# Two weight stages of a decoder trunk: w_out with its recurrent half first in three tiles, w_pg with four accumulators

## The chip, the cores and the metric

The kernel runs on one core of one Trainium2 chip. The metric is the device time of one execution in microseconds. TensorE is called PE, VectorE DVE, ScalarE ACT, GpSimd POOL and SyncE SP, as in the profile.

## The reference, cut to what matters

One layer, 264 tokens (256 of a prompt, 8 of a sample group), width 2048:

```python
c = silu(layernorm(causal_dw_conv(u)))            # channels 0 to 1023
r_out = rg_lru(lx) * gelu(l_gate)                 # channels 1024 to 2047
h = h + concatenate([c, r_out], axis=-1) @ w_out
h = h + hier_moe(rmsnorm(h, norm2_g), ...)        # 32 experts, top 2 of 8 in one of 4 groups
gate = sigmoid(rmsnorm(h, ple_norm_g) @ w_pg + b_pg)
h = h + gate * (p @ w_ple)
y = rmsnorm(h, final_g)
```

The change lies in the product with w_out and in the product with w_pg, both 2048 x 2048.

## The kernel before, in words

The stages follow each other: the input product w_in (PE tiles 0 to 31), w_out (tiles 32 to 47, `CT_OUT`), router, w_ple, 32 experts, w_pg (`CT_PG`), final norm. Every engine's program is written out by hand, in order, with semaphores between engines.

w_out and w_pg are worked alike. Output is made in 16 tiles of 128 channels. The weights of tile t (128 x 2048 floats, 1 MB) are loaded by SP into one of four slots (`lo_slot`), ACT rounds them into another of four slots (`round_weights`, L1105, counted by `w_hi_ready`), and DVE leaves the rest, weight minus rounded weight, in the first slot (`rest_weights`, L1420, counted by `w_lo_ready`). The activations are split the same way (`x_hi`, `mix_lo` for w_out; `gx_hi`, `gx_lo` for w_pg). A tile is then 48 matmuls, three for each of 16 blocks k: high x high, high x low, low x high (`split_product`, L790 to L792). Accumulators are PSUM banks n % 3. SP loads weight tile t once the product of tile t-4 is done (L473, L509).

w_out: `MIX_ORDER` takes the recurrent blocks 8 to 14, then the conformer blocks 0 to 7, then 15. For blocks 0 to 7 ACT still has to do `silu` (L1148) and then the rounding (L1160), and DVE the low part (L1458); PE waits for `mix_lo_ready` block by block in tile 0. DVE's `rest_weights(2)` stands behind all 16 low parts. After each tile DVE adds it to hT (L1479) and PE does `logits` (L811) and `turn_rows` (L637, L638).

w_pg: tile m = 0 and 1 are done in passes (all high x high, then low x high, then high x low; L762, L766, L772). ACT rounds tile 16 (m = 0), makes `gx_hi` with tile 17's rounding in between, rounds tile 18, then makes 16 squares (L1238) that POOL adds up (L553). PE sums them over the channels (L1029, `sum3_full`), from which DVE and ACT make the norm's factor `rb3`. Then, for each m, DVE has one iteration: z = accumulator x rb3 (L1703, `z3_ready`); `rest_weights(KD + m + 3)`, which waits for ACT's rounding, which stands behind ACT's sigmoid (L1252) of z; z x pleT (L1707); hT + z (L1708, `h3_ready`); `take_back(m - 3)` (L1694, L1696, `y_taken`). PE after split_product m does `turn_back(m - 3)`, the transposes (L637, L638) that take_back reads; turn_back(b) waits for h3 of b and, from b = 2 on, for `y_taken` b - 1, that is take_back(b - 2). ACT also squares the new hT (L1248), and POOL adds the squares up.

The lines of the w_pg stage on PE before are these:

```python
for m in range(2, KD):
    if m >= 3:
        pe.wait_ge(z3_ready, m - 3 + 1)
    split_product(KD + m, CT_PG + m, GATE_ORDER, None)
    if m >= 3:
        turn_back(m - 3)
```

Of the kernel before, what the change touches and what calls it, by code (L numbers as in the profile page):

```python
# [17 lines left out]
TOK = SEQ + NB  # L18
# [21 lines left out]
MIX_ORDER = list(range(TC, KD - 1)) + list(range(TC)) + [KD - 1]  # L40
# [62 lines left out]
def build(nc, a, o):  # L103
# [265 lines left out]
    w_lo_ready = sem("w_lo_ready")  # L369
    mix_hi_ready = sem("mix_hi_ready")  # L370
# [148 lines left out]
    def _(pool):  # L519
# [113 lines left out]
    def _(pe):  # L633
# [123 lines left out]

        def high_high(t, n, ks, ready):
            for i, k in enumerate(ks):
                if ready:  # L760
                    pe.wait_ge(ready, i + 1)
                pe.matmul(ps[:, n % 3, 0:TOK], ring_r[:, hi_slot(t), k, :], gate_hi(t)[:, k, :], start=(i == 0), stop=False)  # L762

        def low_high(t, n, ks):
            for k in ks:
                pe.matmul(ps[:, n % 3, 0:TOK], ring_r[:, lo_slot(t), k, :], gate_hi(t)[:, k, :], start=False, stop=False)  # L766

        def high_low(t, n, ks, ready):
# [13 lines left out]
        def split_product(t, n, ks, ready):  # L782

            out = ps[:, n % 3, 0:TOK]
            pe.wait_ge(w_lo_ready, t + 1)
            for i, k in enumerate(ks):
                if ready:
                    pe.wait_ge(ready, i + 1)
                w_hi, w_lo = ring_r[:, hi_slot(t), k, :], ring_r[:, lo_slot(t), k, :]
                pe.matmul(out, w_hi, gate_hi(t)[:, k, :], start=(i == 0), stop=False)  # L790
                pe.matmul(out, w_hi, gate_lo(t)[:, k, :], start=False, stop=False)  # L791
                mm = pe.matmul(out, w_lo, gate_hi(t)[:, k, :], start=False, stop=(i == KD - 1))  # L792
            mm.then_inc(acc_full, 1)
# [29 lines left out]

        for m in range(KD):
            n = CT_OUT + m
            if m < 3:
                pe.wait_ge(acc_free, n - 3 + 1)
            else:
                pe.wait_ge(h_added, m - 3 + 1)
            split_product(m, n, MIX_ORDER, mix_lo_ready if m == 0 else None)  # L830
            if m >= 1:
                logits(m - 1)
                turn_rows(m - 1)
            if m in (2, 4, 6):
                turn_tails(m // 2 - 1)
            if m in (8, 9):

                k = m - 8
                if k == 0:
                    pe.wait_ge(p_loaded, 32)  # L840
                    pe.wait_ge(tail_taken, 3)
                else:
                    pe.wait_ge(pT_ready, 1)
                for c in range(3):
                    r = ROWS[c]
                    last = pe.transpose(ps[:, 5, c * P:c * P + r], prow[0:r, c, k * P:(k + 1) * P], ident[0:r, 0:r])
                last.then_inc(p_turned, 1)
# [174 lines left out]
        pe.wait_ge(w_hi_ready, KD + 2)  # L1022
# [5 lines left out]
        pe.wait_ge(sq3_summed, KD)  # L1028
        pe.matmul(ps[:, 7, 0:TOK], ones[:, :], acc3[:, :], start=True, stop=True).then_inc(sum3_full, 1)  # L1029
        for m in range(2, KD):  # L1030
            if m >= 3:
                pe.wait_ge(z3_ready, m - 3 + 1)
            split_product(KD + m, CT_PG + m, GATE_ORDER, None)
            if m >= 3:
                turn_back(m - 3)
        turn_back(KD - 3)
        turn_back(KD - 2)
        turn_back(KD - 1)
# [9 lines left out]
    def _(act):  # L1048
# [178 lines left out]
        for i, k in enumerate(GATE_ORDER):  # L1227
# [22 lines left out]
        for m in range(KD):  # L1250
# [3 lines left out]
            if m + 3 < KD:  # L1254
                round_weights(KD + m + 3)
# [12 lines left out]
    def _(dve):  # L1268
# [191 lines left out]
        rest_weights(2)  # L1460
# [214 lines left out]
        rest_weights(KD)  # L1675
        for i, k in enumerate(GATE_ORDER):
# [22 lines left out]
        for m in range(KD):  # L1699
# [9 lines left out]
            if m >= 3:  # L1709
                take_back(m - 3)  # L1710
# [69 lines left out]
```

## Time and profile before

| | |
|---|---|
| median of 3 runs | 1581.22 us (1580.81 to 1581.28) |
| the profiled execution's own time | 1583.43 us |
| its span, first to last instruction | 1581.6 us |
| PE busy | 1482.3 us, 94% |
| DVE, ACT, POOL busy | 618.0, 249.5, 129.2 us |
| w_out stage, first to last tile | from 285.7 to about 412 us |
| experts | from about 432 to 1444 us |
| w_pg stage and the end | from about 1444 us |

All positions are microseconds from the span's start. A row of the timeline gives start, length, engine, line, operation, output and inputs with shapes, how often, and in brackets how long the engine sat idle before it and what ended that. A run of equal instructions is merged into one row. A row of a table of stretches gives, for each engine, busy time and number of instructions, then the granted TensorE clock as a share of full speed and what the DMA moved. Matmuls are pipelined, so that the distance between two starts tells their pace, not the length shown.

### The profile page before, as it was taken

Reading aid. Unit: us, or ns where it says so; the run is one execution under the profiler, and the core shown is the slowest. Engines: PE = TensorE matmul, PEld = TensorE weight load, DVE = VectorE, ACT = ScalarE, POOL = GpSimd, SP = SyncE. Lnnn points to the kernel's source line nnn. Section 1 sums busy time; section 2 is a strip of 40 time slices with the busy share of each in tenths; the row PEclk is TensorE's granted clock in tenths of the full one; section 3 lists DMA queues with packets and bytes.
Section 4 is the critical chain, followed back from the end, with each engine's and each line's share of the span. In section 5 each row is a group of like instructions: output and inputs, shape, how many; then the busy total and the mean of one; then the engine's idle time right before and its main releaser. Section 6 shows DMA issues by size and latency. Waiting matters only on the chain.

```text
span 1581.6 us, 18598 instructions
## 1 busy us (share of the span) xinstructions
PE 1482.3 (94%) x7733; PEld 850.6 (54%) x7733; DVE 618.0 (39%) x1230; ACT 249.5 (16%) x414; POOL 129.2 (8%) x116
## 2 busy tenths in 40 slices
PE   6999998999999999999999999999999999998996
PEld 4888887788763333333433433333343333335885
DVE  4698743644552222222222222222222222226665
ACT  3100155633300000000000000000000000004432
POOL 2000000233000000000000000000000000002332
PEclk9999999999999999999999999999999999998998
DMA  9845340345469999999999999999999999991551
GB/s 288 261 147 199 106 107 1 87 134 154 182 260 422 421 421 421 418 411 409 413 405 414 413 403 414 413 409 407 413 413 403 412 415 409 408 372 46 160 160 56
DMA packets 149855, 482.70 MB, mean 305 GB/s; under 512 B 8313, under 2 KB 90785, under 8 KB 99682
## 3 DMA queue, kind: packets, MB, share of 16 engines
q1 hardware_dynamic: 148426, 475.46, 77.6%
q0 software_dynamic: 912, 2.89, 0.6%
q10 hardware_dynamic: 432, 3.15, 0.5%
q8 instruction: 62, 1.02, 0.3%
q14 instruction: 23, 0.19, 0.0%
HBM read 479.06 MB, written 3.42 MB: 305 GB/s over the span
## 4 chain that ended last, share of the span: by engine, by line
PE 85%; DVE 7%; ACT 4%; issue 2%; POOL 1%; DMA 1%; DVEq 0%; ACTq 0%; SPq 0%; POOLq 0%
PE ps L936 29%; PE ps L962 16%; PE ps L662 15%; PE ps L916 8%; PE ps L953 3%; PE ps L943 2%; PE ps L790 2%; PE ps L792 2%; PE ps L791 2%; ACT ring_r L1105 2%; DVE ring_r L1420 2%; DVE hT L1645 1%; DVE sgl L1631 1%; POOL acc L553 1%; PE ps L638 1%
## 5 line engine op out<-in xcount | busy, mean ns | idle before, releaser
L936 PE MATMUL ps<-ring,xwin 128*64 128x512 f32 x1984 | 451.4, 597 | 0.0
L1645 DVE TENSOR_TENSOR hT<-hT,ps 128x528 f32<-128x528 f32 x256 | 168.7, 700 | 394.6 <-PE ps L916 394.6
L936 PEld LDWEIGHTS ps<-ring,xwin 128*64 128x64 f32 x1984 | 133.2, 137 | 263.2 <-issue 263.2
L962 PE MATMUL ps<-ring,hid 128*64 128x512 f32 x1024 | 259.1, 664 | 0.0
L662 PE MATMUL ps<-xT,ring 128*128 128x264 f32 x1024 | 234.7, 391 | 0.0
L662 PEld LDWEIGHTS ps<-xT,ring 128*128 128x128 f32 x1024 | 197.6, 193 | 34.7
L962 PEld LDWEIGHTS ps<-ring,hid 128*64 128x64 f32 x1024 | 78.2, 157 | 153.4 <-issue 152.7
L916 PE MATMUL ps<-sel,ysb 64*128 64x264 f32 x1024 | 149.1, 409 | 1.5 <-DVE ysb L1637 0.8
L916 PEld LDWEIGHTS ps<-sel,ysb 64*128 64x128 f32 x1024 | 87.9, 186 | 112.4 <-issue 100.6
L1637 DVE COPY ysb<-ps 128x512 f32<-128x512 f32 x32 | 22.1, 692 | 287.1 <-PE ps L962 287.1
L1200 ACT ACTIVATE sgl<-ps 64x512 f32<-64x512 f32 x32 | 18.9, 589 | 548.2 <-PE ps L936 548.2
L605 POOL COPY xwin<-xTs 128x1024 f32 x31 | 32.4, 1047 | 879.9 <-PE ps L936 857.0
L1280 DVE SCALAR_TENSOR_TENSOR mix<-U,vT,mix 128x256 f32<-128x256 f32 x240 | 95.3, 475 | 0.0
L1420 DVE TENSOR_TENSOR ring_r<-ring,ring_r 128x2048 fp32r<-128x2048 f32 x32 | 73.7, 2306 | 33.9 <-ACT ring_r L1105 33.3
L943 PE MATMUL ps<-ident,sgl 64*128 64x64 f32 x256 | 35.3, 278 | 54.0 <-DVE sgl L1631 54.0
L790 PE MATMUL ps<-x_hi,ring_r 128*128 128x264 f32 x256 | 76.0, 297 | 3.4 <-DVE mix_lo L1458 3.3
L792 PE MATMUL ps<-x_hi,ring_r 128*128 128x264 f32 x256 | 73.3, 286 | 0.0
L791 PE MATMUL ps<-mix_lo,ring_r 128*128 128x264 f32 x256 | 73.2, 286 | 0.0
L1105 ACT ACTIVATE ring_r<-ring 128x2048 fp32r<-128x2048 f32 x32 | 61.0, 1906 | 47.1 <-DMA ring<-in_w_out_dram 46.7
L790 PE MATMUL ps<-gx_hi,ring_r 128*128 128x264 f32 x224 | 66.0, 295 | 2.2 <-DVE ring_r L1420 2.2
L943 PEld LDWEIGHTS ps<-ident,sgl 64*128 64x128 f32 x256 | 30.8, 187 | 67.1 <-DVE sgl L1631 67.1
L791 PE MATMUL ps<-gx_lo,ring_r 128*128 128x264 f32 x224 | 64.2, 287 | 0.0
(318 smaller groups left out, 1271.8 us busy)
## 6 DMA issues: line engine op xcount, KB each, us to landing
ring<-in_w_gate_dram SPq DMA_DIRECT2D x128, 1024.0 KB, 10.8
ring<-in_w_up_dram SPq DMA_DIRECT2D x128, 1024.0 KB, 9.1
ring<-in_w_down_dram SPq DMA_DIRECT2D x128, 1024.0 KB, 8.1
ring<-in_w_in_dram SPq DMA_DIRECT2D x32, 512.0 KB, 8.7
ring<-in_w_in_dram SPq DMA_DIRECT2D x16, 1024.0 KB, 8.0
ring<-in_w_out_dram SPq DMA_DIRECT2D x16, 1024.0 KB, 5.9
ring<-in_w_pg_dram SPq DMA_DIRECT2D x16, 1024.0 KB, 6.0
ring<-in_w_ple_dram SPq DMA_DIRECT2D x2, 1024.0 KB, 5.8
```

What stands on the lines that cost most here:

```text
L662: mm = pe.matmul(ps[:, n % 3, 0:TOK], w, rhs[:, k, :], start=(k == 0), stop=(k == kt - 1))
L790: pe.matmul(out, w_hi, gate_hi(t)[:, k, :], start=(i == 0), stop=False)
L791: pe.matmul(out, w_hi, gate_lo(t)[:, k, :], start=False, stop=False)
L792: mm = pe.matmul(out, w_lo, gate_hi(t)[:, k, :], start=False, stop=(i == KD - 1))
L916: mm = pe.matmul(ps[:, 4 + 2 * (u % 2) + half, 0:TOK], ysb[rows, b, i * P:(i + 1) * P], sel[rows, :], start=True, stop=True)
L936: mm = pe.matmul(ps[part * WIN:(part + 1) * WIN, 0, :], window(k), weights(2 * j + part)[:, kk * F:(kk + 1) * F], start=(k == 0), stop=(k ...
L943: mm = pe.matmul(ps[:, 1, t * WIN:(t + 1) * WIN], sgl[WIN:2 * WIN, t * P:(t + 1) * P], ident[WIN:2 * WIN, WIN:2 * WIN], start=True, stop=True)
L962: mm = pe.matmul(ps[half * WIN:(half + 1) * WIN, 2 + b, :], hid[:, t, :], weights(8 + t)[:, q * 512:(q + 1) * 512], start=(t == 0), stop=( ...
L1105: act.activation(ring_r[:, hi_slot(t), :, :].rearrange("p k c -> p (k c)"), ring[:, lo_slot(t), :], ACT.Copy).then_inc(w_hi_ready, 1)
L1280: return dve.scalar_tensor_tensor(out=out, in0=in0, scalar=s, in1=in1, op0=op0, op1=op1)
L1420: dve.tensor_tensor(lo, ring[:, lo_slot(t), :], hi.bitcast(F32), ALU.subtract).then_inc(w_lo_ready, 1)
L1645: dve.tensor_tensor(pair, pair, ps[:, b:b + 2, 0:TOK], ALU.add).then_inc(sems["added"], 1)
```

## The change

In w_out, PE takes the blocks 8 to 14 (`MIX_FIRST`) of tiles 0, 1 and 2 first, in passes, in three accumulators, and then the remaining blocks (`MIX_REST`) tile by tile. DVE does rest_weights(2) after the first seven low parts. In w_pg there are four accumulators (banks 0, 1, 2, 6). POOL rounds weight tiles 17 and 18 before the squares; ACT rounds tile 19 among the squares, and tile 20 and later after the sigmoid of m = t - 20. DVE does the rests of 16 and 17 before the low parts, of 18 and 19 after them, and in iteration m of the rest ahead of tile m + 4 comes after z x pleT and hT + z. The sum over the squares stands behind product m = 3. turn_back starts behind product 4, with two behind product 5 (`BACK`).

```diff
+POOL_ROUNDS = (KD + 1, KD + 2)
+BACK = {4: (0,), 5: (1, 2), **{m: (m - 3,) for m in range(6, KD)}}
+MIX_FIRST = list(range(TC, KD - 1))
+MIX_REST = list(range(TC)) + [KD - 1]
...
@@ pool
         pool.sem_inc(extra_done, 1)
+        for i, t in enumerate(POOL_ROUNDS):
+            pool.wait_ge(*landed("tile", t))
+            pool.wait_ge(main["used"], used_chunk(NCH - 9 + t % PG_SLOTS))
+            pool.tensor_copy(ring_r[:, hi_slot(t), :, :].rearrange("p k c -> p (k c)"), ring[:, lo_slot(t), :])\
+                .then_inc(w_hi_pool, 1)
...
@@ tensor
+        def acc_bank(n):
+            return n % 3 if n < CT_PG else (0, 1, 2, 6)[(n - CT_PG) % 4]
...
+        for m in range(2):
+            pe.wait_ge(acc_free, CT_OUT + m - 3 + 1)
+            first_high(m, CT_OUT + m)
+        for m in range(2):
+            first_low(m, CT_OUT + m)
+        pe.wait_ge(acc_free, CT_OUT)
+        first_high(2, CT_OUT + 2)
+        first_low(2, CT_OUT + 2)
         for m in range(KD):
             n = CT_OUT + m
             if m < 3:
-                pe.wait_ge(acc_free, n - 3 + 1)
+                rest_product(m, n)
             else:
                 pe.wait_ge(h_added, m - 3 + 1)
-            split_product(m, n, MIX_ORDER, mix_lo_ready if m == 0 else None)
+                split_product(m, n, MIX_ORDER, None)
...
-        pe.wait_ge(sq3_summed, KD)
-        pe.matmul(ps[:, 7, 0:TOK], ones[:, :], acc3[:, :], start=True, stop=True).then_inc(sum3_full, 1)
         for m in range(2, KD):
-            if m >= 3:
-                pe.wait_ge(z3_ready, m - 3 + 1)
+            if m >= 4:
+                pe.wait_ge(z3_ready, m - 4 + 1)
             split_product(KD + m, CT_PG + m, GATE_ORDER, None)
-            if m >= 3:
-                turn_back(m - 3)
-        turn_back(KD - 3)
-        turn_back(KD - 2)
-        turn_back(KD - 1)
+            if m == 3:
+                pe.wait_ge(sq3_summed, KD)
+                pe.matmul(ps[:, 7, 0:TOK], ones[:, :], acc3[:, :], start=True, stop=True).then_inc(sum3_full, 1)
+            for b in BACK.get(m, ()):
+                turn_back(b)
+        for m in range(KD - 3, KD):
+            turn_back(m)
...
@@ scalar
-            if i == 3:
-                round_weights(KD + 1)
         act.dma_start(ring[:, FING_SLOT, :], a["final_g"].partition_broadcast(P)).then_inc(fing_loaded, 16)
-        round_weights(KD + 2)
         for i, k in enumerate(GATE_ORDER):
             if i >= 2:
                 act.wait_ge(sq3_summed, i - 1)
             act.activation(sqt[:, i % 2, :], hT[:, k, :], ACT.Square).then_inc(sq3_ready, 1)
+            if i == 3:
+                round_weights(KD + 3)
...
-            if m + 3 < KD:
-                round_weights(KD + m + 3)
+            if m + 4 < KD:
+                round_weights(KD + m + 4)
...
@@ vector
+            if i == len(MIX_FIRST) - 1:
+                rest_weights(2)
...
         rest_weights(KD)
+        rest_weights(KD + 1)
         for i, k in enumerate(GATE_ORDER):
             dve.wait_ge(gx_hi_ready, i + 1)
             stt(gx_lo[:, k, :], hT[:, k, :], vT[:, V_PN + k:V_PN + k + 1], gx_hi[:, k, :].bitcast(F32),
                 ALU.mult, ALU.subtract).then_inc(gx_lo_ready, 1)
-            if i == 3:
-                rest_weights(KD + 1)
         rest_weights(KD + 2)
+        rest_weights(KD + 3)
...
-            dve.tensor_tensor(zt[:, m % 2, :], ps[:, (CT_PG + m) % 3, 0:TOK], rb3[:, :], ALU.mult).then_inc(z3_ready, 1)
-            if m + 3 < KD:
-                rest_weights(KD + m + 3)
+            dve.tensor_tensor(zt[:, m % 2, :], ps[:, (0, 1, 2, 6)[m % 4], 0:TOK], rb3[:, :], ALU.mult).then_inc(z3_ready, 1)
             dve.wait_ge(sig_ready, m + 1)
             link(dve.tensor_tensor(zt[:, m % 2, :], zt[:, m % 2, :], pleT[:, m, :], ALU.mult))
             dve.tensor_tensor(hT[:, m, :], hT[:, m, :], zt[:, m % 2, :], ALU.add).then_inc(h3_ready, 1)
-            if m >= 3:
-                take_back(m - 3)
+            if m + 4 < KD:
+                rest_weights(KD + m + 4)
+            for b in BACK.get(m, ()):
+                take_back(b)
```

`first_high`, `first_low` and `rest_product` are the three parts of a tile's product: high x high and low x high over blocks 8 to 14; high x low over them; all three over the other blocks.

## Rows read from the trace of the kernel before

**Rows 1.** Chain that ended last, from 1436 us on, shares by line
```profile
by line: ACT ring_r L1105 20.7%; DVE ring_r L1420 20.4%; POOL acc L553 9.1%; issue 8.3%; DVE zt L1707 7.8%; ACT gx_hi L1229 4.3%; DVE zt L1703 3.6%; DVE ring L1694 3.1%; PE ps L790 1.5%; DVE ring L1696 1.4%; PE ps L792 1.3%; PE ps L791 1.3%
```

**Rows 2.** Timeline, the first three w_out tiles, ACT, DVE and PE
```profile
284.67 2.29 ACT L1160 ACTIVATE x_hi<-mix 128x264 fp32r<-128x264 f32 x7
285.16 2.49 DVE L1458 TENSOR_TENSOR mix_lo<-mix,x_hi 128x264 fp32r<-128x264 f32 x7
...
285.73 0.36 PE L790 MATMUL ps<-x_hi,ring_r 128*128 128x264 f32 x1 [1.47 <-DVE mix_lo L1458]
...
290.21 0.39 PE L790 MATMUL ps<-x_hi,ring_r 128*128 128x264 f32 x1 [1.68 <-DVE mix_lo L1458]
...
295.63 2.29 DVE L1420 TENSOR_TENSOR ring_r<-ring,ring_r 128x2048 fp32r<-128x2048 f32 x1
...
302.23 0.64 PE L811 MATMUL ps<-hT,wr 128*36 128x264 f32 x2
...
303.47 0.39 PE L790 MATMUL ps<-x_hi,ring_r 128*128 128x264 f32 x1
...
309.53 0.64 PE L811 MATMUL ps<-hT,wr 128*36 128x264 f32 x2
```

**Rows 3.** Table of stretches, the start of w_out, PE alone
```profile
285.70:290.20 4.50, 2.81 (x21) 1.00 0.23 60
...
291.10:294.40 3.30, 3.30 (x13) 0.50 0.00 0
```

**Rows 4.** Timeline, low parts and their matmuls in w_pg
```profile
1447.24 1.70 DVE L1280 SCALAR_TENSOR_TENSOR gx_lo<-hT,vT,gx_hi 128x264 fp32r<-128x264 f32 x4
...
1451.06 10.54 DVE L1280 SCALAR_TENSOR_TENSOR gx_lo<-hT,vT,gx_hi 128x264 fp32r<-128x264 f32 x12
...
1462.70 2.88 PE L772 MATMUL ps<-gx_lo,ring_r 128*128 128x264 f32 x13
```

**Rows 5.** Chain in order of time, from the sum to the rest
```profile
1466.79 0.72 PE ps L1029 x2
...
1470.30 0.44 DVE zt L1703
...
1471.29 1.81 ACT ring_r L1105
1473.12 2.29 DVE ring_r L1420
```

**Rows 6.** Timeline, PE in w_pg
```profile
1475.56 0.56 PE L790 MATMUL ps<-gx_hi,ring_r 128*128 128x264 f32 x1 [2.25 <-DVE ring_r L1420]
...
1483.01 0.38 PE L637 MATMUL ps<-ident,hT 128*128 128x128 f32 x2
...
1483.64 0.39 PE L790 MATMUL ps<-gx_hi,ring_r 128*128 128x264 f32 x1
...
1489.55 0.38 PE L637 MATMUL ps<-ident,hT 128*128 128x128 f32 x2
...
1564.47 0.38 PE L637 MATMUL ps<-ident,hT 128*128 128x128 f32 x2
```

**Rows 7.** Table of stretches, w_pg: PE, PEld, DVE, ACT, POOL, clock, DMA
```profile
1475.60:1479.00 3.40, 3.40 (x16) 3.40 (x17) 0.98 (x4) 2.40 (x3) 0.00 (x0) 0.52 0.88 250
```

**Rows 8.** The page, POOL's window copies
```profile
L605 POOL COPY xwin<-xTs 128x1024 f32 x31 | 32.4, 1047 | 879.9 <-PE ps L936 857.0
```

**Rows 9.** Timeline, POOL's additions beside DVE's work
```profile
310.60 2.42 POOL L553 TENSOR_TENSOR acc<-acc,sqh 128x264 f32<-128x264 f32 x1 [3.40 <-ACT sqh L1180]
...
312.33 0.48 DVE L1468 TENSOR_TENSOR h_lo<-ps,h_hi 128x128 fp32r<-128x128 f32 x2
...
1533.20 2.55 POOL L553 TENSOR_TENSOR acc<-acc,sqt 128x264 f32<-128x264 f32 x1 [4.36 <-ACT sqt L1248]
...
1535.05 0.98 DVE L1707 TENSOR_TENSOR zt<-zt,pleT 128x264 f32<-128x264 f32 x1
```

**Rows 10.** The page, DMA issues of w_pg, median us to landing
```profile
ring<-in_w_pg_dram SPq DMA_DIRECT2D x16, 1024.0 KB, 6.0
```

More of the change, by code:

```diff
@@ L39 @@
 PG_SLOTS = 4
-MIX_ORDER = list(range(TC, KD - 1)) + list(range(TC)) + [KD - 1]
+POOL_ROUNDS = (KD + 1, KD + 2)
+BACK = {4: (0,), 5: (1, 2), **{m: (m - 3,) for m in range(6, KD)}}
+MIX_FIRST = list(range(TC, KD - 1))
+MIX_REST = list(range(TC)) + [KD - 1]
+MIX_ORDER = MIX_FIRST + MIX_REST
 GATE_ORDER = [k for u in range(KD // 2) for k in (u, u + KD // 2)]
@@ L369, in build @@
     w_lo_ready = sem("w_lo_ready")
+    w_hi_pool = sem("w_hi_pool")
     mix_hi_ready = sem("mix_hi_ready")
@@ L761, in high_high @@
                     pe.wait_ge(ready, i + 1)
-                pe.matmul(ps[:, n % 3, 0:TOK], ring_r[:, hi_slot(t), k, :], gate_hi(t)[:, k, :], start=(i == 0), stop=False)
+                pe.matmul(ps[:, acc_bank(n), 0:TOK], ring_r[:, hi_slot(t), k, :], gate_hi(t)[:, k, :], start=(i == 0), stop=False)
         def low_high(t, n, ks):
             for k in ks:
-                pe.matmul(ps[:, n % 3, 0:TOK], ring_r[:, lo_slot(t), k, :], gate_hi(t)[:, k, :], start=False, stop=False)
+                pe.matmul(ps[:, acc_bank(n), 0:TOK], ring_r[:, lo_slot(t), k, :], gate_hi(t)[:, k, :], start=False, stop=False)
         def high_low(t, n, ks, ready):
@@ L771, in high_low @@
                     pe.wait_ge(ready, i + 1)
-                mm = pe.matmul(ps[:, n % 3, 0:TOK], ring_r[:, hi_slot(t), k, :], gate_lo(t)[:, k, :], start=False,
+                mm = pe.matmul(ps[:, acc_bank(n), 0:TOK], ring_r[:, hi_slot(t), k, :], gate_lo(t)[:, k, :], start=False,
                                stop=(i == KD - 1))
@@ L782, in split_product @@
         def split_product(t, n, ks, ready):
-            out = ps[:, n % 3, 0:TOK]
+            out = ps[:, acc_bank(n), 0:TOK]
             pe.wait_ge(w_lo_ready, t + 1)
@@ L792, in split_product, with first_high, first_low, rest_product @@
                 mm = pe.matmul(out, w_lo, gate_hi(t)[:, k, :], start=False, stop=(i == KD - 1))
+            mm.then_inc(acc_full, 1)
+        def first_high(t, n):
+            pe.wait_ge(w_hi_ready, t + 1)
+            for i, k in enumerate(MIX_FIRST):
+                if t == 0:
+                    pe.wait_ge(mix_hi_ready, i + 1)
+                pe.matmul(ps[:, acc_bank(n), 0:TOK], ring_r[:, hi_slot(t), k, :], x_hi[:, k, :], start=(i == 0), stop=False)
+            pe.wait_ge(w_lo_ready, t + 1)
+            for k in MIX_FIRST:
+                pe.matmul(ps[:, acc_bank(n), 0:TOK], ring_r[:, lo_slot(t), k, :], x_hi[:, k, :], start=False, stop=False)
+        def first_low(t, n):
+            for i, k in enumerate(MIX_FIRST):
+                if t == 0:
+                    pe.wait_ge(mix_lo_ready, i + 1)
+                pe.matmul(ps[:, acc_bank(n), 0:TOK], ring_r[:, hi_slot(t), k, :], mix_lo[:, k, :], start=False, stop=False)
+        def rest_product(t, n):
+            out = ps[:, acc_bank(n), 0:TOK]
+            for i, k in enumerate(MIX_REST):
+                if t == 0:
+                    pe.wait_ge(mix_lo_ready, len(MIX_FIRST) + i + 1)
+                w_hi, w_lo = ring_r[:, hi_slot(t), k, :], ring_r[:, lo_slot(t), k, :]
+                pe.matmul(out, w_hi, x_hi[:, k, :], start=False, stop=False)
+                pe.matmul(out, w_hi, mix_lo[:, k, :], start=False, stop=False)
+                mm = pe.matmul(out, w_lo, x_hi[:, k, :], start=False, stop=(i == len(MIX_REST) - 1))
             mm.then_inc(acc_full, 1)
@@ L1021, in _ @@
         low_high(KD, CT_PG, GATE_ORDER)
-        pe.wait_ge(w_hi_ready, KD + 2)
+        pe.wait_ge(w_hi_pool, 1)
         high_high(KD + 1, CT_PG + 1, GATE_ORDER, None)
@@ L1415, in rest_weights @@
         def rest_weights(t):
-            dve.wait_ge(w_hi_ready, t + 1)
+            if t in POOL_ROUNDS:
+                dve.wait_ge(w_hi_pool, POOL_ROUNDS.index(t) + 1)
+            else:
+                dve.wait_ge(w_hi_ready, t + 1 if t <= KD else t + 1 - len(POOL_ROUNDS))
             lo = ring_r[:, lo_slot(t), :, :].rearrange("p k c -> p (k c)")
@@ L1459, in _ @@
                 .then_inc(mix_lo_ready, 1)
-        rest_weights(2)
+            if i == len(MIX_FIRST) - 1:
+                rest_weights(2)
         def rows_low(m):
```

## The prediction

> **What bounds the kernel now.** I read the page first: PE is busy for 94% of the span, so time is won or lost where PE waits, or where it runs at the lower clock. Then I read the two stages that the change touches, first by the chain of work that ended last, then by the timeline of each engine, then by a table of stretches for the granted clock.
>
> At the start of w_out PE does 21 matmuls of blocks 8 to 14 and then idles, because ACT's silu and rounding and DVE's low part give one conformer block after another [rows 2]. After that hole the granted clock is 0.50, the 1.2 GHz level, from 291.1 to 294.4 us; before it, it was 1.00 [rows 3]. The first three products run from 285.73 to 309.5 us.
>
> In w_pg the chain is not PE's: ACT's rounding and DVE's rest of the weights hold 41% of it, POOL's additions 9% [rows 1]. PE could do a tile in 6.54 us (1483.01 to 1489.55, 48 matmuls and one turn_back) [rows 6], but from 1489.55 to 1564.47 it did 11 tiles in 74.9 us, 6.81 each: DVE's iteration (z, wait for sigmoid and rounding, rest, three additions, take_back) is longer than PE's. Before that PE stood 2.25 us in front of product m = 3, because rest_weights(19) came only behind z(0) [rows 5, 6].
>
> **The terms.** A product of 48 matmuls at the high clock takes 5.91 us (1483.64 to 1489.55), a turn_back 0.63, together 6.54 [rows 6]. A product after a stall takes 1483.01 - 1475.56 = 7.45 us; its extra 1.5 us is the 3.4 us at granted clock 0.52 [rows 6, 7]. From the start of the sum's matmul to z(0) it is 1470.30 - 1466.79 = 3.5 us, and from z(0) to the end of the rest that follows it 1475.41 - 1470.30 = 5.1 us [rows 5]. This last term is the core of a DVE iteration in both kernels: z, ACT's sigmoid, ACT's rounding, DVE's rest.
>
> **w_out.** PE no longer waits for low parts at its start, but for x_hi, whose first comes about 0.4 us after 284.67, so PE begins near 285.2. Its first seven matmuls are paced by ACT, 2.29 / 7 = 0.33 each against 0.12, which costs 1.3 us [rows 2]. Then 56 matmuls of the first blocks are there without a wait (DVE's seven low parts end at 287.65, its rest of tile 2 now at about 289.9 instead of 297.8), which lasts to about 294. DVE had the low parts of the other nine blocks done by 295.63, when its rest of tile 2 began; PE asks for the last of them 8 x 0.37 us after 294, at 297, so they come in time [rows 2]. The sum: 285.2 + 1.3 + 3 x 5.91 + 1.24 (logits and turn_rows after tile 1, 302.23 to 303.47) = 305.4 us for the end of product 2, against 309.5 [rows 2]. The gain is 4.1 us. What is late next: tile 0 ends 1 us later, so the load of weight tile 4 is issued at about 297.7; with 6.0 us of landing [rows 10], 1.8 of rounding and 2.3 of rest [rows 5] it stands near 308, while PE needs it only after product 3, near 314.5. Queued behind that rest on DVE is hT + product 2, done near 308.8, before PE's turn_rows(2) asks for it. If ACT's slow first seven matmuls let the clock fall, 1.5 us of it goes; the gain cannot be above 4.9 us, the whole excess of 23.8 us over 3 x 5.91 + 1.24. Bounds 2.4 to 4.5, I take 4.1. Its cover is in PE's own queue, so it is passed on whole: what follows (router chain, expert loads gated by these tiles) starts from PE.
>
> **POOL's two roundings** are 128 x 2048; the nearest row is a copy of 128 x 1024 in 1.05 us [rows 8], so about 2.1 us each, doubled if they are blocked. They wait for their loads and for slots that expert 31 has used, so they run during expert 31, and PE asks for the first only at its third pass, after 1448. Behind them on POOL stand only the squares. What they can cost is DVE's gate of expert 31: 0 to 1 us, I take 0.
>
> **w_pg up to product 3.** ACT is rid of two roundings of 1.8 us [rows 5], so gx_hi is complete 1.8 us earlier and the squares begin 3.6 us earlier, with tile 19's rounding put between. DVE now does both rests, the first until 1447.2 as before, the second until 1449.5, and then 16 low parts. Four of them without POOL beside them took 1.70 us, 12 with it 10.54, 0.88 each [rows 4]. So 16 take 13 to 14 us and end at about 1463.3 instead of 1461.5. PE has them paced, its clock is at 0.50 again, and the last 16 matmuls take 16 x 0.22 = 3.5 us [rows 4] (2.0 at the high clock): product m = 2 begins at about 1466.8 (1465.2 at best), against 1467.15. The wait for the sum, which began at 1466.79 [rows 5], is gone from here, but the low parts take its place. Products 2 and 3 need the rests of 18 and 19, ready at 1465.6 and 1468, and run through: 1466.8 + 2 x 5.91 = 1478.6.
>
> **w_pg, product 4** (positions here leave w_out's gain aside)**.** Only now comes the sum's matmul, and z(0) is at 1478.6 + 3.5 = 1482.1, 11.8 us later than before. Product 4 waits for z3 of 0 and, worse, for the rest of tile 20. ACT rounds that tile behind the sigmoid of z(0), DVE leaves its rest behind hT + z(0). So it stands at 1482.1 + 5.1 = 1487.2, and PE has idled for 7.9 us since its sum. The fourth accumulator doesn't help: the weights are not there.
>
> **w_pg, turn_back(2).** Products 4 and 5 take 7.45 + 0.63 + 5.91 from 1487.3, to 1501.3; turn_back(1) to 1501.9. turn_back(2) then waits for take_back(0). That one stands in DVE's iteration 4, behind rest_weights(24), and DVE has been working off iterations 0 to 3 since z(0), 5.1 us each, since z(m + 1) stands behind the rest of tile m + 4. So take_back(0) ends at 1482.1 + 5 x 5.1 + 0.6 = 1508.2, and PE idles another 6.3 us. Product 6 ends at 1508.2 + 0.1 + 0.63 + 7.45 = 1516.4, again with 1.5 us of low clock. (The low clock of product 4 costs nothing: it lies inside this wait.)
>
> Does POOL lengthen these iterations? After a rest, POOL's waiting addition goes first and DVE's next operation takes 0.98 instead of 0.43, where both its inputs are in SBUF; where one is in PSUM (312.33, while POOL's addition ran from 310.60 to 313.02) it isn't lengthened [rows 9]. In the new order the operation after the rest is z or take_back, which read PSUM, so I take 0; the upper bound is 4 x 0.55 = 2.2 us. The Trainium skill, page "SBUF — State Buffer", section "Who interferes with whom", says that a DVE instruction with at most one SBUF input does not contend with GpSimd. The two rows agree; by the opposite reading the sum would be 2 us more.
>
> **w_pg, the rest.** From there PE is the slower one. DVE's iteration, 5.1 + 0.6, is shorter than PE's 6.54. A load is issued at the end of product m and lands 6.0 us later [rows 10], then rounding 1.8, rest 2.3, take_back 0.6 to 1.1: DVE's z(m + 1) runs at most 5 us behind PE, and turn_back asks for take_back(m - 5) about 2 us after it is done. Nine tiles at 6.54 to 6.6: 59.1, so the last product ends at 1575.5, against 1564.47 [rows 6]. The end behind it is the same in both kernels: turn_backs 12 to 15, last sum, last scaling. w_pg: +11.0 us. Where DVE's shorter iteration gives back: 11 x 0.27 = 3 us, already in this.
>
> **Sum.** -4.1 + 11.0 = +6.9 us. On the span of 1581.6 that is 1588.5. The profiled execution took 1583.43, the median of the three runs is 1581.22; the predicted median is 1581.2 + 6.9 = 1588.1.
>
> **Rivals.**
> B. The wait of turn_back(2) isn't there, only that of product 4 (if DVE got through its iterations much faster than 5.1 us, or PE were held elsewhere by as much). Then product 6 ends at 1501.9 + 0.63 + 5.91 = 1508.4, the last at 1567.5: +3.0 - 4.1 = -1.1, 1580.1. For it: nothing but the promise of slack; against: the order in the code, and 5.1 us from a row. 0.09.
> C. Faster: products 4 and on never wait, PE goes at its own pace from 1466.8: 14 x 5.91 + 12 x 0.63 + 0.7 = 91.0, last product at 1557.8, -6.7 - 4.1 = -10.8, 1570.4. It decides on the rest of tile 20: if it were ready before 1479. Against it: its rounding stands behind z(0) [rows 5]. Anything that makes the kernel faster by 3.2 us needs both stalls together (14.2 us, and 1.5 of clock) to be under about 6. 0.04.
> D. More than forecast: POOL does lengthen every iteration (+2.2), the clock falls in w_out (+1.5), the roundings on POOL hold expert 31's gate (+1): 1590 to 1593. 0.12.
> A. The forecast, 1585 to 1590.5: 0.75.
>
> **Range.** Low: product 2 at 1465.2 (-1.6), w_out 4.5 (-0.4), no low clock after the second stall (-1.5) give 1584.6. High: D's 1592.8. I give 1584.4 to 1592.8; B and C and ends beyond hold less than 0.2. A measurement of this kernel can tell about 0.2% (3.2 us) from no change: slower 0.87, same 0.09, faster 0.04.
>
> **What the changed profile would show.** w_out: PE with no idle over 0.5 us between 287 and 305, clock 1.00, tile 2's product ending near 305.4. Against the start of w_pg, on PE: a wait of about 8 us for DVE's rest (L1420's successor) in front of product 4; a wait of about 6 us at the transposes between products 5 and 6, released by DVE's take_back, followed by a few us at half clock; then a period of 6.5 to 6.6 us. DVE: five iterations of 5.1 us after z(0). The prediction is wrong if the second wait is missing or short, if z(0) comes before 1476 in the place where I have 1482.1 (all these positions less 4.1 us in the changed kernel, for w_out), or if periods after product 6 stay at 6.9.

## The result and the profile after

The changed kernel takes 1588.93 us, median of 5 runs (1588.44 to 1589.5), against 1581.28 (5 runs, 1580.81 to 1582.05): a ratio of 1.0047, 95% interval 1.0033 to 1.0062, or 7.65 us more. The forecast was 1588.1 us, 6.9 more. The profiled execution took 1588.82 us, with a span of 1587.1 against 1581.6.

From the page of the kernel after: the span, the busy time (us, share, instructions), and the group of the first matmul of each block k of a w_pg product (busy us, mean ns, then idle time before it and what ended it):

```profile
span 1587.1 us, 18599 instructions
PE 1480.3 (93%) x7733; PEld 849.2 (54%) x7733; DVE 614.9 (39%) x1230; ACT 246.0 (16%) x412; POOL 130.9 (8%) x118
L803 PE MATMUL ps<-gx_hi,ring_r 128*128 128x264 f32 x224 | 67.1, 300 | 8.0 <-DVE ring_r L1471 8.0
```

PE is busy for 2 us less and the span is 5.5 us longer, so PE stands idle for 7.5 us more. The waits from 1430 us on (engine and line that wait, what for, us in total, times, longest) hold two large ones on PE:

```profile
PE ps L803 <- DVE ring_r L1471: 8.0, 1, 8.0
PE ps L647 <- DVE ring L1748: 7.3, 2, 5.4
```

The first is product 4 waiting for the rest of tile 20, the second (5.4 us of it) is turn_back(2) waiting for take_back(0); the other 1.9 us is the end's, as before. The timeline of DVE after, from the low parts to take_back(0):

```profile
1440.04 4.70 DVE L1471 TENSOR_TENSOR ring_r<-ring,ring_r 128x2048 fp32r<-128x2048 f32 x2 [0.44 <-issue]
1444.66 13.46 DVE L1328 SCALAR_TENSOR_TENSOR gx_lo<-hT,vT,gx_hi 128x264 fp32r<-128x264 f32 x16
1458.05 5.03 DVE L1471 TENSOR_TENSOR ring_r<-ring,ring_r 128x2048 fp32r<-128x2048 f32 x2
1475.16 0.43 DVE L1736 TENSOR_SCALAR rbt<-ps 128x264 f32<-128x264 f32 x1 [12.08 <-PE ps L1083]
...
1477.92 0.43 DVE L1755 TENSOR_TENSOR zt<-ps,rb 128x264 f32<-128x264 f32 x1
1478.93 0.43 DVE L1757 TENSOR_TENSOR zt<-zt,pleT 128x264 f32<-128x264 f32 x1 [0.58 <-ACT zt L1300]
1479.40 0.43 DVE L1758 TENSOR_TENSOR hT<-hT,zt 128x264 f32<-128x264 f32 x1
1480.73 2.29 DVE L1471 TENSOR_TENSOR ring_r<-ring,ring_r 128x2048 fp32r<-128x2048 f32 x1 [0.90 <-ACT ring_r L1154]
1482.94 0.42 DVE L1755 TENSOR_TENSOR zt<-ps,rb 128x264 f32<-128x264 f32 x1
...
1503.02 0.42 DVE L1746 TENSOR_TENSOR ring<-ps,ring 128x256 f32<-128x256 f32 x1
1503.36 0.27 DVE L1748 TENSOR_TENSOR ring<-ps,ring 8x128 f32<-8x128 f32 x1
```

DVE stands idle for 12.08 us before the sum, then does z(0) and, one behind the other, iterations of 5.02 us (z at 1477.92, 1482.94, 1487.96, 1492.98, 1498.00). take_back(0) ends at 1503.63. On PE after:

```profile
1483.17 0.56 PE L803 MATMUL ps<-gx_hi,ring_r 128*128 128x264 f32 x1 [8.05 <-DVE ring_r L1471]
...
1491.09 0.38 PE L647 MATMUL ps<-ident,hT 128*128 128x128 f32 x2
...
1503.77 0.66 PE L647 MATMUL ps<-ident,hT 128*128 128x128 f32 x2 [5.44 <-DVE ring L1748]
...
1571.26 0.38 PE L647 MATMUL ps<-ident,hT 128*128 128x128 f32 x2
```

These stand where before had one idle of 2.25 us in front of product 3 and then 11 periods of 6.81 us [rows 6]. The stretches of the kernel after (busy time and count for PE, PEld, DVE, ACT, POOL, then granted clock, DMA share, GB/s) show the clock behind both waits:

```profile
1475.00:1482.90 7.90, 0.12 (x1) 0.00 (x0) 5.71 (x6) 4.02 (x4) 0.00 (x0) 0.65 0.47 133
1483.00:1486.50 3.50, 3.33 (x15) 3.36 (x16) 1.99 (x5) 2.63 (x3) 0.41 (x1) 0.50 0.02 5
1503.70:1508.00 4.30, 4.23 (x18) 3.50 (x19) 2.78 (x4) 2.63 (x3) 1.30 (x2) 0.50 0.02 6
1508.00:1571.00 63.00, 63.00 (x502) 59.52 (x502) 32.68 (x56) 18.92 (x24) 18.82 (x10) 1.00 0.37 101
```

From 1508 to 1571 us PE is never idle, at full clock; behind that only the 1.9 us of the end are left. So the loss arises between 1475 and 1508.

Where the difference of the spans comes from, by marks that both traces have (us):

| from, to | before | after | after - before | forecast |
|---|---|---|---|---|
| start to the last gelu of w_in | 284.29 | 283.01 | -1.28 | 0 |
| to the logits of w_out's tile 1 | 25.24 | 22.76 | -2.48 | -4.1 |
| to the silu of expert 0 | 150.21 | 150.22 | 0.0 | 0 |
| to the silu of expert 1 | 42.34 | 40.72 | -1.62 | 0 |
| to the silu of expert 31 | 921.85 | 922.23 | +0.38 | 0 |
| to z(0) | 46.37 | 58.98 | +12.61 | +11.8 |
| from z(0) to z(15) | 94.37 | 93.53 | -0.84 | about -0.8 |
| to the end | 16.93 | 15.65 | -1.28 | 0 |

The first row is not the change's: the same mark lies between 281.7 and 284.4 us in the profiles of e1 to e10, whatever the kernel. That profiled execution of before, 1583.43 us, also lies 2.15 above its median, that of after at its median, which is why the spans differ by 5.5 and the medians by 7.65. Without the first row the two traces differ by 6.8 us; the 0.9 us from there to 7.65 stand in no row of one profile each.

### The profile page after: what moved, and what is told of

The parts are those of the page before. It is cut to its first block, busy times and chain, and to the rows that moved or that the text cites. A ratio compares the mean times of both kernels' runs of the same rounds, so it can differ in the third digit from the quotient of the medians.

```text
span 1587.1 us, 18599 instructions
## 1 busy us (share of the span) xinstructions
PE 1480.3 (93%) x7733; PEld 849.2 (54%) x7733; DVE 614.9 (39%) x1230; ACT 246.0 (16%) x412; POOL 130.9 (8%) x118
## 4 chain that ended last, share of the span: by engine, by line
PE 90%; DVE 5%; issue 2%; ACT 2%; DMA 1%; DVEq 0%; SPq 0%; ACTq 0%
PE ps L985 29%; PE ps L1011 16%; PE ps L672 15%; PE ps L965 8%; PE ps L803 3%; PE ps L805 3%; PE ps L804 3%; PE ps L1002 3%; PE ps L992 2%; DVE hT L1697 2%; DVE sgl L1683 1%; PE ps L648 1%; DVE gx_lo L1328 1%; PE ps L686 1%; ACT ring_r L1154 1%
## 5 line engine op out<-in xcount | busy, mean ns | idle before, releaser
L803 PE MATMUL ps<-gx_hi,ring_r 128*128 128x264 f32 x224 | 67.1, 300 | 8.0 <-DVE ring_r L1471 8.0
L1154 ACT ACTIVATE ring_r<-ring 128x2048 fp32r<-128x2048 f32 x30 | 57.3, 1909 | 53.2 <-DMA ring<-in_w_out_dram 43.5
L805 PE MATMUL ps<-gx_hi,ring_r 128*128 128x264 f32 x224 | 65.3, 291 | 0.0
L803 PE MATMUL ps<-x_hi,ring_r 128*128 128x264 f32 x208 | 60.6, 291 | 0.0
L805 PE MATMUL ps<-x_hi,ring_r 128*128 128x264 f32 x208 | 59.1, 284 | 0.0
```

Source lines behind the costliest of these rows:

```text
L1154: act.activation(ring_r[:, hi_slot(t), :, :].rearrange("p k c -> p (k c)"), ring[:, lo_slot(t), :], ACT.Copy).then_inc(w_hi_ready, 1)
```

## The experiments

The theory: two waits stand in a row. The sum behind product 3 sets z(0) 12 us late; that starves product 4, and DVE's backlog of late iterations then starves turn_back(2). The rival to each part: the wait isn't the sum's but the weights' or the accumulators', or the two waits are one and the same delay, so that taking one away takes both. The runs before of the same chips lie at 1581.6 to 1582.3 us; each difference is against these, unless it says otherwise. Between medians of two kernels from different chips some tenths of a us mean nothing: before itself differs by up to 1.0 us from chip to chip (1581.28 to 1582.28). Fillers, in some kernels, are matmuls on a bank that nobody reads.

**Each half alone.** e1: the passes of w_out, with DVE's rest_weights(2) after the first seven low parts, and w_pg as before:

```diff
+        for m in range(2):
+            first_high(m, CT_OUT + m)
+        for m in range(2):
+            first_low(m, CT_OUT + m)
...
+            if i == len(MIX_FIRST) - 1:
+                rest_weights(2)
```

> The kernel before with the w_out part of the change alone. Theory: w_out is worth 2.5 to 4 us and the w_pg part costs the rest; the profile of the changed kernel shows every expert's silu 3.7 to 5.4 us earlier than before, of which 1.3 us was already there before w_out began. So about 1577.5 us (1576 to 1579). Rival: most of that earlier position was there by chance and w_out is worth nothing: 1580 to 1582.

Measured 1578.72 against 1581.6: 0.9980 (0.9971 to 0.9989), -2.9 us. w_out's start takes 22.75 us, as in the full change, and the path from expert 31 to z(15) 140.75 as in before. That is inside the expected 1576 to 1579. Its trace has the 2.5 us of w_out and 1.6 at expert 0 (40.71 us for 42.34), and gives back 0.8 in the experts behind (922.67 us from the silu of expert 1 to that of 31, against 921.85).

e2: the same part undone in the changed kernel; w_pg as changed:

```diff
-        for m in range(2):
-            first_high(m, CT_OUT + m)
...
+            split_product(m, n, MIX_ORDER, mix_lo_ready if m == 0 else None)
```

> The kernel before with the w_pg part of the change alone. Theory: the two waits of PE (8.0 us for the rest of tile 20, 5.4 us for take_back(0)) and the lower clock after the second cost about 10.5 to 11 us net: 1592 us (1590.5 to 1593.5). Rival: w_out's part is what makes the w_pg part slow (they share nothing but time), then less than 1589.

Measured 1592.72: 1.0071 (1.0057 to 1.0085), +11.1 us. The waits are 8.0 and 5.5 us. The halves add up: -2.9 + 11.1 = 8.2, against 7.65. w_pg is the loss, w_out a small gain.

**The second wait alone.** e3: DVE does take_back(0) in iteration 3 and take_back(1) in iteration 4, instead of both an iteration later; PE's order is untouched:

```diff
+TAKE = {3: (0,), 4: (1,), 5: (2,), **{m: (m - 3,) for m in range(6, KD)}}
...
-            for b in BACK.get(m, ()):
+            for b in TAKE.get(m, ()):
                 take_back(b)
```

> The changed kernel, with DVE's take_back of 0, 1, 2 one iteration earlier (iterations 3, 4, 5), PE's order as it is. Theory: take_back(0) ends 4 x 5.0 + 0.6 us after z(0), at about 1498.6, and PE asks for it at 1498.3; the wait of 5.4 us shrinks to under 1 us and the 1.6 us of lower clock after it go: 1588.9 - 6.5 = 1582.4 us (1581.5 to 1584). The wait before product 4 stays at 8 us. Rival: DVE is simply behind, and the wait moves to a later transpose or product: 1587 to 1589.

Measured 1582.08: 1.0006 (0.9997 to 1.0015), which is 6.85 us under the changed kernel. The timeline of PE in e3 at turn_back(2):

```profile
1497.89 0.41 PE L648 MATMUL ps<-ident,hT 128*128 128x128 f32 x2 [0.46 <-DVE ring L1749]
```

5.44 us of wait have become 0.46, the wait of 8.0 before product 4 stays, and the transposes take 0.41 instead of 0.66: the half clock behind the wait is gone too. 5.0 + 1.5 = 6.5, of 6.85. The second wait hangs on DVE's order, and it goes without the first one.

**The first wait alone.** e4: the sum's matmul ahead of product 2, as in before:

```diff
         high_low(KD + 1, CT_PG + 1, GATE_ORDER, None)
+        pe.wait_ge(sq3_summed, KD)
+        pe.matmul(ps[:, 7, 0:TOK], ones[:, :], acc3[:, :], start=True, stop=True).then_inc(sum3_full, 1)
         for m in range(2, KD):
...
-            if m == 3:
-                pe.wait_ge(sq3_summed, KD)
-                pe.matmul(ps[:, 7, 0:TOK], ones[:, :], acc3[:, :], start=True, stop=True).then_inc(sum3_full, 1)
```

> The changed kernel, with the sum over the squares ahead of product m = 2, where the kernel before had it. POOL's additions end at 1458.7, before PE needs the sum at 1462.3, so it costs no wait. Theory: z(0) comes at about 1466 instead of 1478, the rest of tile 20 at 1471, before product 4 needs it at 1475: the wait of 8 us is gone; turn_back(2) still waits about 3.5 us for take_back(0), with 1.6 us of lower clock. The last product ends 12.5 us earlier: 1576.4 us (1574.5 to 1578.5). Rival: the first wait is only a symptom, DVE's loop is the bound, and the gain is under 6 us: 1583 or more.

Measured 1578.03: 0.9976 (0.9967 to 0.9985), 10.9 us under the changed kernel. z(0) comes 47.02 us after the silu of expert 31 instead of 58.98. Of the waits of e4 from 1430 us on, this is PE's largest, and none on a weight tile of products 2 to 15 is left:

```profile
PE ps L647 <- DVE ring L1747: 5.7, 2, 3.8
```

The sum waits for nobody there (POOL's additions are done). The second wait is still there, 3.8 us at turn_back(2) and 1.9 at the end: take_back(0) still stands five iterations behind z(0).

**Both.** e5 has the two edits of e3 and e4.

> Both repairs together: the sum ahead of product 2 and take_back(0), (1), (2) in DVE's iterations 3, 4, 5. Theory: neither wait is left; against the run with the early sum alone the remaining 3.8 us at the transposes and 1.6 us of lower clock go: 1578.0 - 5.4 = 1572.6 us (1571 to 1574.5), with products at a period of 6.5 to 6.6 us from 4 to 15. Rival: a third bound stands right behind (DVE's iterations or the loads), so that the two repairs don't add: over 1575.5.

Measured 1572.17 against 1582.13: 0.9935 (0.9922 to 0.9949), -10.0 us. Only the wait of the end is left on PE's transposes:

```profile
PE ps L648 <- DVE ring L1748: 1.9, 1, 1.9
```

With two edits the kernel now does what rival C of the prediction supposed of the change as it stood, that PE goes at its own pace from product 4 on; C's figure was 1570.4.

**Is the first wait the weights' or the sum's?** e6: ACT rounds tile 20, and DVE leaves its rest, ahead of z(0); the sum stays behind product 3:

```diff
+        round_weights(KD + 4)
         act.wait_ge(ms_ready, 3)
...
         rest_weights(KD + 3)
+        rest_weights(KD + 4)
         dve.wait_ge(sum3_full, 1)
```

> The changed kernel, with tile 20's rounding and rest ahead of the sum instead of behind z(0); the sum stays behind product 3. This takes away most of the wait before product 4 alone (8.0 to about 3.3 us, what is left is z(0)). Theory: the wait before product 4 lies in front of the wait for take_back(0), which is set by z(0) and DVE's five iterations; only the 3.0 us that iteration 0 loses with its rest are gained: 1588.9 - 3.1 = 1585.8 us (1584.5 to 1587). The wait at turn_back(2) grows from 5.4 to about 7 us. Rival: the waits add up, 4.7 us and more are gained: 1584.2 or less.

Measured 1586.87: 1.0026 (1.0017 to 1.0035), or 4.7 us above before of the same chip where the changed kernel stands 7.65 above its own: 2.9 us gained, for 3.1 expected (2.1 between the two medians, which are from different chips). Two rows of PE's timeline in e6:

```profile
1479.91 0.59 PE L803 MATMUL ps<-gx_hi,ring_r 128*128 128x264 f32 x1 [3.28 <-DVE zt L1757]
...
1502.09 0.66 PE L647 MATMUL ps<-ident,hT 128*128 128x128 f32 x2 [6.45 <-DVE ring L1750]
```

The wait of 8.05 for tile 20 has become one of 3.28 for z(0), which frees the accumulator, so that this one comes next behind the weights. The 4.8 us saved here don't reach the end: turn_back(2) starts at 22.7 us after z(0) (1479.43), where it was 25.9 in the changed kernel. Iteration 0 is rid of a rounding and a rest, 3.2 us, and that is the whole gain in this stretch (z(15) comes 149.2 us after the silu of expert 31, against 152.5); the length of DVE's backlog sets it, not the first wait. The weights alone don't cure the loss.

**w_out's half clock.** e7: the changed kernel with 64-column fillers after each of tile 0's first seven matmuls and four of 128 columns ahead of them:

```diff
+                if t == 0:
+                    pe.matmul(ps[:, 5, 0:P // 2], ones[:, :], ones[:, 0:P // 2], start=True, stop=True)
...
+        for _ in range(4):
+            pe.matmul(ps[:, 5, 0:P], ones[:, :], ones[:, :], start=True, stop=True)
```

> The changed kernel, with matmuls that nobody reads put where w_out's first seven matmuls wait for ACT's x_hi: four of 128 columns ahead, one of 64 columns behind each of the seven (bank 5). Theory: in every run with the w_out part PE ran at granted clock 0.50 for about 3.4 us from 2 us after its start (22.76 us from the last gelu of w_in to the logits of tile 1, where the prediction had 21.1); with PE busy there the clock stays at 1.00 and w_out is 1.6 us shorter: 1587.3 us (1586 to 1588), 21.1 to 21.4 us in the trace. Rival: the clock falls for the wait ahead of the stage in any case, no change or slower: 22.8 us in the trace, 1588.5 or more.

Measured 1589.2: 1.0042 (1.0028 to 1.0056), 7.1 us above before, for 7.65 in the changed kernel, so no difference that the runs can tell. The expected 1586 to 1588 is missed; the time is the rival's, but the rival's reason, that the clock falls there in any case, is not what happened. Stretches of the changed kernel, then of e7:

```profile
284.00:286.10 2.10, 2.10 (x9) 1.40 (x9) 2.10 (x7) 2.08 (x7) 1.26 (x2) 0.99 0.24 31
286.10:287.50 1.40, 1.40 (x9) 1.40 (x8) 1.40 (x2) 1.39 (x2) 0.00 (x0) 0.50 0.38 146
287.50:289.40 1.90, 1.90 (x11) 1.90 (x10) 1.55 (x3) 1.90 (x6) 0.00 (x0) 0.50 0.00 0
289.40:291.00 1.60, 1.60 (x14) 1.60 (x14) 0.84 (x3) 1.60 (x5) 0.00 (x0) 0.98 0.00 0
```

```profile
284.00:286.00 2.00, 1.92 (x18) 1.75 (x16) 1.86 (x6) 2.00 (x8) 1.13 (x2) 1.00 0.00 0
286.00:290.00 4.00, 4.00 (x36) 4.00 (x35) 3.64 (x6) 3.97 (x8) 0.13 (x1) 1.00 0.23 68
```

The half clock from 286.1 to 289.4 is gone, and w_out's start takes 21.67 us instead of 22.76. The fillers have a price of their own: the first seven matmuls take 2.41 us with them (284.56 to 286.97) and 2.01 without (283.95 to 285.96), so that the fall itself cost about 1.5 us. But the 1.1 us don't reach the end: the step from expert 0 to expert 1 takes 42.34 us again, as in before, not 40.72. In both, PE waits 1.34 us for the gated hidden values of expert 0; in the changed kernel the clock stays at 1.00 behind it, in before and e7 it falls to 0.50. The row of the timeline and the stretch in before:

```profile
474.06 1.10 PE L943 MATMUL ps<-ident,sgl 64*128 64x64 f32 x8 [1.34 <-DVE sgl L1631]
```

```profile
475.60:478.60 3.00, 3.00 (x11) 1.40 (x11) 0.03 (x1) 0.39 (x1) 0.69 (x1) 0.50 1.00 421
```

and the same place in the changed kernel:

```profile
470.32 1.10 PE L992 MATMUL ps<-ident,sgl 64*128 64x64 f32 x8 [1.34 <-DVE sgl L1683]
```

```profile
471.00:475.00 4.00, 4.00 (x24) 2.08 (x25) 0.42 (x1) 0.39 (x1) 1.54 (x2) 1.00 1.01 424
```

**Is the fourth accumulator worth anything?** e8 is e5 with three banks:

```diff
-            return n % 3 if n < CT_PG else (0, 1, 2, 6)[(n - CT_PG) % 4]
+            return n % 3
...
-            if m >= 4:
-                pe.wait_ge(z3_ready, m - 4 + 1)
+            if m >= 3:
+                pe.wait_ge(z3_ready, m - 3 + 1)
```

> The kernel with both repairs, but with three accumulators in w_pg as before (product m waits for z of m - 3). Theory: the fourth accumulator is worth nothing once z(0) is early: z of m - 3 is ready some us before product m begins for every m, so within 0.5 us of the kernel with both repairs. Rival: it is what lets DVE run 5 us behind; then PE waits for z at each product and it is 3 us or more slower.

Measured 1571.44: 0.9933 (0.9919 to 0.9947), e5's time within what the runs can tell. Once z(0) is early, three are enough. What POOL's two roundings and DVE's new order are worth by themselves no run separates.

**The half clock behind a short wait.** e9 is before with six 128-column fillers in front of expert 0's wait:

```diff
+            if sems is main and e == 0:
+                for _ in range(6):
+                    pe.matmul(ps[:, 2, 0:P], ones[:, :], ones[:, :], start=True, stop=True)
             pe.wait_ge(sems["gated"], e + 1)
```

> The kernel before, with six matmuls of 128 columns that nobody reads in expert 0, where PE waits 1.3 us for DVE's gated product (472 to 474 us; bank 2). In the kernel before the granted clock falls to 0.5 for 3.4 us right after that wait (475.2 to 478.6), in the changed kernel it doesn't, and the stretch from expert 0's silu to expert 1's is 42.34 against 40.72 us. Theory: the fall hangs on that idle time; with PE busy there it stays away and the kernel is 1.6 us shorter: 1580 us against 1581.6 (1579 to 1581), silu to silu 40.7 us. Rival: the filler changes nothing or the fall moves to the next gap: 42.3 us, no difference.

Measured 1579.6 against 1582.23: 0.9983 (0.9974 to 0.9992), -2.6 us. Expert 0 to 1 takes 40.71 instead of 42.34 us, and expert 1 to 2, without a filler of its own, 29.13 instead of 30.76. PE waits 1.70 us in expert 1 in both kernels; from 506 to 508 us the clock is 0.52 in before, and in e9 it is 1.00 from 496 to 511 us. The two experts give 3.3 us in the trace, of 2.6 between the medians: the expectation had 1.6. e10 is e8 with the fillers of e7 and e9.

> The kernel with both repairs and three accumulators, with the fillers in w_out's first seven matmuls and in expert 0. Theory: both falls of the clock are then gone at once: w_out 1.1 us shorter (21.67 instead of 22.75 us, as the run with w_out's filler), expert 0 stays at 40.7: 1571.4 - 1.1 = 1570.3 us (1569.3 to 1571.5). Rival: the two falls are tied by more than idle time, one of them comes back in another gap: 1571.4 or more.

Measured 1568.76: 0.9911 (0.9895 to 0.9926), -13.5 us. That is below the expected range: 2.7 us under e8 instead of 1.1, because here too expert 1 to 2 takes 29.13 us, which the expectation left out (1.1 + 1.6 = 2.7).

Expert 1 to 2 at 29.13 was the hint: from there on an expert of before takes 30.72 to 30.76. The wait that recurs, from 800 to 1200 us of before, and then two stretches of before, one behind such a wait and one over most experts:

```profile
PE ps L943 <- DVE sgl L1631: 22.1, 13, 1.7
```

```profile
935.00:940.00 5.00, 4.84 (x22) 3.20 (x24) 0.53 (x2) 0.39 (x1) 0.00 (x0) 0.66 1.02 423
...
500.00:1400.00 900.00, 849.08 (x4154) 345.95 (x4152) 230.15 (x410) 46.75 (x89) 30.37 (x29) 0.94 1.00 412
```

e12 is before with fillers in all experts, e11 is e10 with them:

```diff
-            if sems is main and e == 0:
-                for _ in range(6):
+            if sems is main:
+                for _ in range(6 if e == 0 else 7):
```

> The kernel with both repairs, three accumulators and the fillers, and now with seven such matmuls in each of the 31 other experts too, where PE waits 1.7 us for DVE's gated product; in the trace of before the granted clock falls after each of these waits (0.66 in the stretch 935 to 940 us) and an expert takes 30.72 us. Theory: the transfers are busy all the time (DMA share 1.00, 412 GB/s from 500 to 1400 us) and soon bound the experts: with 12.6 MB per expert at the 426 GB/s of the best stretches an expert can't go below 29.5 us, so at most 31 x 1.2 = 37 us and more likely a few us are gained: 1555 to 1567 us. Rival 1: every expert gets the 1.6 us that expert 0 and 1 got: 1520 us. Rival 2: nothing is gained, the loads are the bound already: 1568 to 1570.

> The kernel before with the fillers in all 32 experts (six in expert 0, seven in each other) and nothing else. In the kernel with both repairs they took the time from 1568.8 to 1537.0 us for 31 experts, 31.8 us. Theory: what they bring is the clock in the experts alone and doesn't depend on the change: with the 2.6 us that expert 0's filler brought before, 1581.6 - 2.6 - 31.8 = 1547 us (1544 to 1550). Rival: part of it came from the loads running ahead in the changed kernel: 1555 or more.

e11: 1536.97 against 1582.28, 0.9712 (0.9699 to 0.9725), -45.3 us. It is 31.8 us under e10, outside the expected 1555 to 1567, though below the 37 us worked out there as the most the loads allow. e12: 1548.2 against 1582.25, 0.9786 (0.9772 to 0.9799), -34.1 us, inside its expectation. The timeline of PE, the stretch and the waits (500 to 1200 us) of e12:

```profile
909.09 1.83 PE L943 MATMUL ps<-ones 128*128 128x128 f32 x14
910.86 1.10 PE L946 MATMUL ps<-ident,sgl 64*128 64x64 f32 x8
911.89 0.83 PE L956 MATMUL ps<-ident,selT 128*128 128x128 f32 x6
912.66 7.09 PE L965 MATMUL ps<-ring,hid 128*64 128x512 f32 x32
```

```profile
500.00:1400.00 900.00, 887.73 (x4733) 395.12 (x4731) 236.70 (x422) 47.80 (x91) 29.32 (x28) 1.00 1.01 419
```

```profile
PE ps L936 <- DMA ring<-in_w_up_dram: 7.5, 26, 1.0
```

The fillers last about as long as the wait did (1.8 us for 1.7), the clock is 1.00 throughout instead of 0.94, and the 32 down products take 7.09 us instead of 8.0. What PE now waits for is the weights' DMA (last row). It shows in the periods of e11: from expert 2 on eleven experts at 29.13 us and eighteen at 30.05 on average (most at 29.8 to 30.0, three at 30.7 to 31.3), against 30.72 in e10, which from expert 2 on is the same without fillers. From the silu of expert 2 to that of expert 31 this is 861.3 us against 891.1, 29.8 of the 31.8 us between e10 and e11. So nothing of the clock's gain is lost to the weights for a third of the experts, and 0.9 of 1.6 us for the others.

The rate of the loads tells why. In e11 and e12 it is 421 GB/s in every stretch from 500 to 1380 us, where before has 421 falling to 408 to 412. An expert needs 12 loads of 1024 KB, 12.6 MB, which is 29.9 us at 421 GB/s. The first experts take less than that, 29.13 us, and PE waits for no load up to 840 us: they use up weights that were loaded ahead. From 840 us on PE waits for loads 40 times, 11.5 us in all, and the experts go at the loads' pace. The DMA share reads 1.00 in before as well, where PE waits for no load: a share of 1.00 did not show that the loads were the bound.

## Why the prediction was right, step by step

**w_out, -4.1 forecast, -2.5 measured.** The step "its first seven matmuls are paced by ACT" held (7 in 2.18 us). The named risk came true: the clock fell to 0.50 from 286.1 to 289.4 us, priced at 1.5; e7 gives back 1.1 of it net, after 0.4 us that its fillers take. So the step that failed is the choice between the two clocks: I took full clock for a PE paced by ACT at 0.31 us a matmul, with no row of before that shows one. What made up for it wasn't in the forecast at all: the half clock after expert 0's wait, 1.62 us, isn't there in the changed kernel. 2.48 + 1.62 = 4.1 is a coincidence. The 1.62 us come with w_out's new start in e1 and are missing in e2, but they are missing in e7 too, which has that start with fillers.

**POOL's two roundings, 0 forecast, 0 found.** They took 1.89 us each, for about 2.1 from the nearest row [rows 8], and stand at 1415.52 and 1419.14, in the shadow of expert 31. DVE's gate of expert 31 came at 1420.94, 2.00 us behind the silu, as in before (1423.93 and 1425.93).

**Product 2 to z(0), +11.8 forecast, +12.6 measured.** Product 2 begins 43.1 us after expert 31's silu for 42.9. Products 2 and 3 take 12.43 us (1462.08 to 1474.51), not 11.82: the first seven matmuls of product 2 still go at 0.22, the clock rising only at 1463.6. I had put the low clock on the low parts and let it end with them. From the sum to z(0), 3.41 for 3.5.

**The wait of product 4, 7.9 forecast, 8.05 measured,** released by DVE's rest of tile 20 as said. e6 shows that z(0), which frees the accumulator, comes right behind it.

**The wait of turn_back(2), 6.3 forecast, 5.44 measured.** take_back(0) ends 25.7 us behind z(0), forecast 26.1, since an iteration takes 5.02 and not 5.1 us, so the wait ends 0.4 us sooner behind z(0). Product 4 takes 7.92 us (1483.17 to 1491.09), not 7.45, as the clock is low for 4.3 us rather than 3.4, so that PE comes to the wait 0.5 us later. 0.4 + 0.5 is what it is shorter by. e3 takes the wait away with an edit on DVE alone, so the working-off of DVE's iterations is shown as its cause.

**POOL beside DVE, 0 forecast, 0 found.** z follows each rest and has one input in PSUM. At 1487.96, 1492.98 and 1498.00 it ran while an operation of POOL's sum ran (these began at 1486.09, 1491.13 and 1496.15 and took 2.2 to 2.6 us), and at 1482.94 with POOL idle: 0.42 us each time. The Trainium skill, page "SBUF — State Buffer", section "Who interferes with whom", says that a DVE instruction with at most one SBUF input does not contend with GpSimd. The trace agrees.

**Product 6 on, 67.2 forecast, 67.5 measured** (1503.77 to 1571.26), with 4.3 us at clock 0.50 and then a period of 6.55 to 6.63.

**The end, 0 forecast, -1.3 measured.** PE's last wait is 1.9 us in both, but the transposes behind it run at full clock after (1574.53 to 1575.87, 1.34 us) and at half clock before (1567.75 to 1570.01, 2.26 us), and the last six small matmuls take 0.79 instead of 1.14. "The end behind it is the same" missed that a wait's price can differ by the clock behind it. Every kernel with the changed w_pg ended in 15.6 to 15.7 us. It was 16.8 to 16.9 in before, e1, e9 and e12, which have the old one. Why the clock fell there only with the old order stays open.

**Luck.** The total came out 0.75 us off on the medians, but four of its parts were off by 0.8 to 1.6 us and cancel: w_out +1.6, expert 0's clock -1.6, z(0) +0.8, the end -1.3. The two waits and their causes were forecast; the closeness of the sum wasn't earned.

**What stays open.** Seven kernels (the changed one, e1, e3, e4, e5, e6 and e8), in which w_out's start took 22.75 us, went through expert 0's wait at full clock; before, e2 and e7 did not, though the wait is 1.34 us in each. Which wait of that length is followed by a fall depends on something upstream that these runs don't isolate.

## What to carry to other kernels

A gain on paper (here more accumulators, and roundings spread over idle engines) can be lost if the value that frees everything behind it is moved back: find the one small operation that starts a loop's chain, here one 0.6 us matmul, and put it as early as its inputs allow. An engine that starts such a loop late works off a backlog in order, so that each later consumer waits for the whole of it; take the consumer's item out of the back of the iteration before widening buffers. Where two waits stand in a row, time each by its own releaser: a gain in front of the second only reaches the end if it moves what ends the second.

## What the runs showed of the hardware

A wait of 1.3 to 1.7 us on PE was followed, in nearly every expert, by some 3 us at the lower granted clock (0.50, 1.2 GHz): 1.6 us an expert, of 30.7. Filling the wait with matmuls that nobody reads kept the clock at 1.00 (2.4 GHz) and gave 34 us on the kernel before and, with the repaired orders, 45 us, down to 1536.97. The share of PE's busy time in the page, 94%, did not show it; the granted clock per stretch did.

The same wait doesn't always have the same price: expert 0's 1.34 us was followed by clock 0.50 in before, e2 and e7 and by 1.00 in the changed kernel and e1, and 1.6 us moved with it. Expert 1's 1.70 us was followed by 0.52 in before and by 1.00 in e9 and e10.

With the clock kept up, the loads became the next bound at 421 GB/s (e11 and e12), 29.9 us an expert.
